# Block products of w_out: seven instead of eight in three of its pairs, on one core

## The reference, cut to what matters

```
y = jnp.concatenate([rmsnorm(y_lru, g_out_lru[i]), rmsnorm(y_attn, g_out_attn[i])], axis=-1)
h = h + y @ w_out[i]
h = h + hier_moe(rmsnorm(h, g_moe[i]), w_rg[i], b_rg[i], w_re[i], b_re[i], w1[i], w3[i], w2[i])
pe = rmsnorm(p[i] @ w_ple[i], g_ple[i])
gate = jax.nn.sigmoid((rmsnorm(h, g_pg[i]) @ w_pg[i]).astype(F32) + b_pg[i].astype(F32))
h = h + (gate * pe.astype(F32)).astype(h.dtype)
```

## Time and profile before

| | |
|---|---|
| time, median of 3 runs | 1372.13 us (1371.0 to 1377.09) |
| time of the profiled execution | 1376.97 us |
| its span on the core | 1375.2 us |
| PE busy | 1094.3 us (80% of the span) |
| DVE busy | 288.5 us (21%) |
| ACT busy | 158.9 us (12%) |
| POOL busy | 53.5 us (4%) |
| bytes read | 473.12 MB, 346 GB/s over the span |

### The profile page before, as it was taken

How to read it: one execution, slowest core, us unless ns; L and a number is a source line. 1 busy time by engine, 2 the same in 40 slices (tenths; PEclk the granted TensorE clock), 3 DMA queues, 4 the chain that set the end, 5 groups by cost and what they waited for, 6 DMA issues and landing times.

```text
span 1375.2 us, 13804 instructions
## 1 busy us (share of the span) xinstructions
PE 1094.3 (80%) x6020; PEld 508.5 (37%) x6020; DVE 288.5 (21%) x443; ACT 158.9 (12%) x315; POOL 53.5 (4%) x66
## 2 busy tenths in 40 slices
PE   8999999999995687666766667666666676899998
PEld 4458887445531233222222223222223222333333
DVE  1204725511341212121221111000000000111116
ACT  1111415002110012000000000000000000110002
POOL 0103100200000002000000000000000000000000
PEclk9999999999898899788898878888878868999999
DMA  9943333364699999999999999999999999999991
GB/s 352 310 153 123 123 123 122 127 248 180 267 384 427 427 427 428 428 430 431 428 426 428 429 426 428 414 427 429 414 428 421 417 427 412 393 397 382 396 353 62
DMA packets 89326, 476.16 MB, mean 346 GB/s; under 512 B 10080, under 2 KB 10224, under 8 KB 67760
## 3 DMA queue, kind: packets, MB, share of 16 engines
q1 hardware_dynamic: 83168, 471.88, 84.8%
q0 software_dynamic: 560, 2.88, 0.6%
q10 hardware_dynamic: 5536, 0.47, 0.3%
HBM read 473.12 MB, written 2.10 MB: 346 GB/s over the span
## 4 chain that ended last, share of the span: by engine, by line
DMA 50%; PE 45%; SPq 3%; DVE 1%; issue 1%; ACT 0%; DVEq 0%
DMA ring<-in_w 49%; PE ps L1457 8%; PE ps L1420 6%; PE ps L1718 6%; PE ps L1798 4%; PE ps L1594 4%; PE ps L1581 4%; PE ps L1895 4%; PE ps L1684 2%; PE ps L1853 2%; SPq L471 1%; PE ps L1677 1%; SPq L462 1%; SPq L389 1%; PE ps L1866 1%
## 5 line engine op out<-in xcount | busy, mean ns | idle before, releaser
L1798 PE MATMUL ps<-ring,area 128*32 128x512 f32 x1024 | 167.7, 805 | 120.7 <-DMA ring<-in_w 119.8
L1718 PE MATMUL ps<-ring,area 128*32 128x512 f32 x976 | 146.4, 719 | 112.5 <-DMA ring<-in_w 112.5
L1209 DVE TENSOR_TENSOR h<-ps,h 128x2048 f32<-128x2048 f32 x32 | 73.3, 2292 | 286.6 <-PE ps L1684 286.6
L1798 PEld LDWEIGHTS ps<-ring,area 128*32 128x32 f32 x1024 | 43.3, 140 | 231.3 <-issue 231.3
L1457 PE MATMUL ps<-hT,ring 128*128 128x256 f32 x512 | 112.9, 380 | 0.0
L1718 PEld LDWEIGHTS ps<-ring,area 128*32 128x32 f32 x976 | 31.4, 122 | 209.0 <-issue 208.6
L1457 PEld LDWEIGHTS ps<-hT,ring 128*128 128x128 f32 x512 | 96.6, 190 | 14.0 <-issue 1.2
L1420 PE MATMUL ps<-ring,hT 128*128 128x512 f32 x192 | 86.0, 608 | 1.1 <-DVE hT L932 1.1
L1895 PE MATMUL ps<-ring,area 128*128 128x512 f32 x176 | 79.8, 595 | 3.5 <-ACT area L896 3.0
L1264 DVE TENSOR_TENSOR hT<-area,ps 128x128 f32<-128x128 f32 x16 | 4.6, 288 | 316.0 <-ACT area L885 316.0
L1677 PE MATMUL ps<-area,hs 128*128 128x128 f32 x512 | 66.8, 286 | 0.5 <-DVE area L1190 0.5
(11 more groups left out here) (285 smaller groups left out, 808.9 us busy)
## 6 DMA issues: line engine op xcount, KB each, us to landing
ring<-in_w SPq DMA_DIRECT2D x126, 2048.0 KB, 20.7
ring<-in_w SPq DMA_DIRECT2D x63, 1024.0 KB, 15.4
ring<-in_w SPq DMA_DIRECT2D x14, 4096.0 KB, 25.2
ring<-in_w_in SPq DMA_DIRECT2D x28, 1024.0 KB, 12.3
ring<-in_w_out SPq DMA_DIRECT2D x16, 1024.0 KB, 7.3
ring<-in_w_pg SPq DMA_DIRECT2D x11, 1024.0 KB, 14.2
area<-in_w SPq DMA_DIRECT2D x2, 2048.0 KB, 14.3
hs<-in_w SPq DMA_DIRECT2D x4, 1024.0 KB, 14.4
```

Of the source, the lines that this page charges most:

```text
L1209: dve.tensor_tensor(h[:, t, :], ps[:, bank:bank + 4, :].rearrange("p b n -> p (b n)"), h[:, t, :], ALU.add).then_inc(acc_done, 1)
L1718: ins = mm(ps[SLOTS * g:SLOTS * g + SLOTS, 0, :], XG[:, b, k, SLOTS * e:SLOTS * e + SLOTS], s[:, D_EXP * kk:D_EXP * kk + D_EXP], start=(k ...
L1798: ins = mm(ps[SLOTS * g:SLOTS * g + SLOTS, 0, :], XG[:, b, k, SLOTS * e:SLOTS * e + SLOTS], s[:, D_EXP * kk:D_EXP * kk + D_EXP], start=(k ...
```

## The change

Three quarters of `w_out` are cut into pairs of column groups: pair 0 is part B with n = 0 and 1, pair 1 part B with n = 2 and 3, pair 2 part A with n = 0 and 1. A pair is a 2 x 2 by 2 x 2 block product (two row tiles t, two halves of 512 inner rows, two column groups), made with Strassen's method (in its form with shared differences) from seven block products of four matmuls each instead of eight. What the products read is made beforehand: four differences of `w_out`'s blocks (128x2048 each) and four of `y`'s (128x512 each). DVE makes those of pairs 0 and 2 (`w_difference`, L1140 to L1147) and all of `y`'s (`y_differences`, L1155 to L1160); POOL makes pair 1's, and the last one of pair 0 (L601 to L615). Each product is added to one, two or three pieces of `h`: 14 additions a pair (`add_products`, L1178; `steps_` lists product, tile, group and the earlier addition to wait for) instead of four (two groups by two tiles). Column groups 2 and 3 of part A stay as they were (L1741).

Line numbers above 1700 on PE, 1130 to 1240 on DVE and 590 to 620 on POOL in this section are those of the changed kernel. SP's load of the first ahead place moves behind the next ring load, since the differences lie in that place until pair 2 is done. A pair's four chunks are freed together, by the first matmul of the next pair. At the end, eight of the logits' blocks of t = 1 are moved ahead of the last transposes (L1757, L1763).

```diff
-                if p_ == 1:
-                    for a in range(2):
-                        expert_load(1, a, ahead_places[a], ahead_loaded[a])
+                if p_ in (1, 2):
+                    expert_load(1, 2 - p_, ahead_places[2 - p_], ahead_loaded[2 - p_])
...
+            pool.wait_ge(chunks_used, WIN_CHUNKS)
+            w_arrived(pool, 1)
+            b11, b12, b22 = w_block(1, 0, 0), w_block(1, 0, 1), w_block(1, 1, 1)
+            pool.tensor_tensor(w_sums[1][:, 0, :], b22, b12, ALU.subtract).then_inc(made_pool, 1)
+            pool.wait_ge(made_pool, 1)
+            pool.tensor_tensor(b12, b12, b11, ALU.subtract).then_inc(made_pool, 1)
+            pool.wait_ge(made_pool, 2)
+            first_b21 = w_last(pool, 0)
+            pool.wait_ge(made_dve, 3)
+            pool.tensor_tensor(first_b21, first_b21, w_sums[0][:, 1, :], ALU.subtract).then_inc(made_pool, 1)
+            pool.tensor_tensor(w_sums[1][:, 1, :], b22, b12, ALU.subtract).then_inc(made_pool, 1)
             pool.wait_ge(lru_act, 4)
...
+            b21 = w_last(pool, 1)
+            pool.wait_ge(made_pool, 4)
+            pool.tensor_tensor(b21, b21, w_sums[1][:, 1, :], ALU.subtract).then_inc(made_pool, 1)
             pool.wait_ge(msBA_ready, 2)
...
+            def y_differences(j, count):
+
+                if j:
+                    dve.wait_ge(products_ps, PRODUCTS + 6)
+                low, high = [y_block(j, t, 0) for t in range(NT)], [y_block(j, t, 1) for t in range(NT)]
+                dve.tensor_tensor(y_sums[:, 0, :, :], low[1], high[1], ALU.add).then_inc(made_dve, 1)
+                dve.tensor_tensor(y_sums[:, 2, :, :], low[0], low[1], ALU.subtract).then_inc(made_dve, 1)
...
+            w_difference(0, 0, 1)
+            w_difference(0, 1, 2)
+            w_difference(0, 2, 3)
+
+            def add_products(j, first, last):
+
+                steps_ = ((0, 0, 0, 0), (0, 0, 1, 0), (0, 1, 0, 0), (0, 1, 1, 0), (1, 0, 0, 1),
+                          (2, 0, 1, 2), (2, 1, 0, 3), (2, 1, 1, 4), (3, 0, 1, 6), (3, 1, 1, 8),
+                          (4, 1, 0, 7), (4, 1, 1, 10), (5, 0, 1, 9), (6, 1, 0, 11))
+                for i, t, n, earlier in steps_[first:last]:
+                    dve.wait_ge(products_ps, PRODUCTS * j + i + 1)
...
+            dve.wait_ge(gates_ps, CB)
+            y_differences(0, 3)
+
 
             dve.wait_ge(gates_ready, CB)
             dve.tensor_tensor(t2, t2, xc, ALU.mult)
...
+            add_products(0, 0, STEPS)
+            w_difference(2, 0, 8)
+            w_difference(2, 1, 9)
+            w_difference(2, 2, 10)
+            dve.wait_ge(lru_act, 4)
+            dve.tensor_reduce(ysum, t1.rearrange("p c t -> p t c"), AX, ALU.add).then_inc(made_dve, 1)
+            add_products(1, 0, 12)
+            dve.wait_ge(ssA_ps, 1)
+            dve.tensor_scalar(ss[:, 4:6], ps[:, 0, 0:NT], 1.0 / D_LRU, EPS, ALU.mult, ALU.add).then_inc(msBA_ready, 1)
+            add_products(1, 12, 13)
+            dve.wait_ge(made_pool, 4 + CB)
+            y_differences(2, 11)
+            add_products(1, 13, STEPS)
             dve.wait_ge(rBA_ready, 2)
...
+            def product(j, i, y, w, frees=0):
+
+                m = PRODUCTS * j + i
+                if 2 <= m < 6:
                     pe_.wait_ge(gates_ready, CB)
-                if n == 3:
-
-                    pe_.wait_ge(hB_ready, 1)
-                    pe_.wait_ge(ysum_ready, 1)
+                elif 6 <= m < 8:
+                    pe_.wait_ge(block_copied, 2 * CB)
+                elif m >= 8:
+                    j_, i_ = divmod(m - 8, PRODUCTS)
+                    pe_.wait_ge(pieces_added, STEPS * j_ + READ_BY[i_])
+                for kk in range(4):
+                    ins = mm(ps[:, product_bank(m), :], y[:, kk, :], w[:, 512 * kk:512 * kk + 512],
+                             start=(kk == 0), stop=(kk == 3))
...
+                product(j, 4, y_sums[:, 2, :, :], w_sums[j][:, 0, :])
+                if j == 1:
+                    pe_.wait_ge(made_dve, 11)
+                    pe_.wait_ge(pieces_added, STEPS)
                     for t in range(NT):
-                        ins = mm(ps[:, 2, t:t + 1], ysum[:, P * t:P * t + P], ones_c[:, 0:1], start=True, stop=True)
+                        ins = mm(ps[:, 0, t:t + 1], ysum[:, P * t:P * t + P], ones_c[:, 0:1], start=True, stop=True)
                     ins.then_inc(ssA_ps, 1)
...
+            pair(0)
+            pair(1)
+            pe_.wait_ge(msBA_ready, 2)
+            pe_.wait_ge(made_pool, 4 + CB)
+            pair(2)
...
+            w_out_A(1, 3)
+            logits(1, 0, 8)
             turn_h(1, 3)
             pe_.wait_ge(xnT_act, 7)
-            logits(1, 0, 12)
+            logits(1, 8, 12)
```

More of the change, by code:

```diff
@@ L352, in ring4, with y_block, w_block, wait_piece @@
             return ring[:, slot, :].rearrange("p (k n) -> p k n", k=4)
+        y_sums = hs_flat[:, 0:2048].rearrange("p (w k m) -> p w k m", w=4, k=4)
+        w_sums = [part(10264, 2 * CH, 2, CH), hT_flat.rearrange("p (w n) -> p w n", w=2), part(10264, 2 * CH, 2, CH)]
+        def y_block(j, t, half):
+            return (yT if j < 2 else gt)[:, 4 * half:4 * half + 4, P * t:P * t + P]
+        def w_block(j, half, n):
+            return ring[:, (pair_chunk(j) + 2 * n + half) % RING, :]
+        def wait_piece(engine, t, n):
+            if n < 2:
+                engine.wait_ge(pieces_added, ADDED - STEPS + WHOLE_BY[t, n])
+            else:
+                engine.wait_ge(h_ready, 2 * t + n - 1)
+        def w_arrived(engine, j):
+            for half, n in ((0, 0), (0, 1), (1, 1)):
+                c = pair_chunk(j) + 2 * n + half
+                engine.wait_ge(loaded[c % RING], 16 * (c // RING + 1))
+        def w_last(engine, j):
+            c = pair_chunk(j) + 1
+            engine.wait_ge(loaded[c % RING], 16 * (c // RING + 1))
+            engine.wait_ge(products_ps, PRODUCTS * j + 2)
+            return w_block(j, 1, 0)
         block = ctx.enter_context(nc.Block())
@@ L1066, in _, with w_difference @@
             dve.tensor_scalar(ss[:, 6:8], ss[:, 6:8], 1.0 / (HEADS * HD), EPS, ALU.mult, ALU.add).then_inc(msBA_ready, 1)
+            def w_difference(j, which, count):
+                b11, b12, b22 = w_block(j, 0, 0), w_block(j, 0, 1), w_block(j, 1, 1)
+                dve.wait_ge(made_dve, count - 1)
+                if which == 0:
+                    w_arrived(dve, j)
+                    ins = dve.tensor_tensor(w_sums[j][:, 0, :], b22, b12, ALU.subtract)
+                elif which == 1:
+                    ins = dve.tensor_tensor(b12, b12, b11, ALU.subtract)
+                elif which == 2:
+                    ins = dve.tensor_tensor(w_sums[j][:, 1, :], b22, b12, ALU.subtract)
+                else:
+                    b21 = w_last(dve, j)
+                    ins = dve.tensor_tensor(b21, b21, w_sums[j][:, 1, :], ALU.subtract)
+                ins.then_inc(made_dve, 1)
@@ new lines, in _ @@
+            w_difference(0, 0, 1)
[7 more added lines that the diff above has]
+                    dve.wait_ge(products_ps, PRODUCTS * j + i + 1)
+                    if earlier or j:
+                        dve.wait_ge(pieces_added, STEPS * j + earlier)
+                    col = 512 * (2 * (j % 2) + n)
+                    piece = h[:, t, col:col + 512]
+                    scale = (6 if j < 2 else 4) + t
+                    dve.scalar_tensor_tensor(out=piece, in0=ps[:, product_bank(PRODUCTS * j + i), :],
+                                             scalar=rstd[:, scale:scale + 1], in1=piece, op0=ALU.mult, op1=ALU.add
+                                             ).then_inc(pieces_added, 1)
@@ L1122, in _ @@
+            dve.wait_ge(pieces_added, ADDED)
+            add_A(0, 2)
+            add_A(0, 3)
             root_mean(0)
@@ new lines, in arrived, with pair @@
+            def arrived(j, half, n):
+                chunk(pair_chunk(j) + 2 * n + half)
+                return w_block(j, half, n)
+            def pair(j):
+                product(j, 0, y_block(j, 0, 0), arrived(j, 0, 0), 4 * (j > 0))
+                product(j, 1, y_block(j, 0, 1), arrived(j, 1, 0))
+                if j == 0:
+                    pe_.wait_ge(made_dve, 7)
+                elif j == 1:
+                    pe_.wait_ge(made_pool, 4)
+                else:
+                    pe_.wait_ge(made_dve, 15)
+                product(j, 2, y_sums[:, 1, :, :], w_sums[j][:, 1, :])
+                product(j, 3, y_sums[:, 0, :, :], arrived(j, 0, 1))
+                product(j, 4, y_sums[:, 2, :, :], w_sums[j][:, 0, :])
+                if j == 1:
+                    pe_.wait_ge(made_dve, 11)
+                    pe_.wait_ge(pieces_added, STEPS)
@@ L1587, in w_out_A @@
-            def w_out_A(t, n):
+                product(j, 5, y_sums[:, 3, :, :], arrived(j, 1, 1))
+                if j == 0:
+                    pe_.wait_ge(made_pool, 3)
+                elif j == 1:
+                    pe_.wait_ge(made_pool, 5 + CB)
+                else:
```

(8 more changed lines are left out.)

157 lines of the change are left out of this document (74 added, 83 removed).

## The result

| | before | after |
|---|---|---|
| time, median of 7 runs | 1372.13 us (1371.0 to 1377.09) | 1378.94 us (1377.77 to 1379.42) |
| ratio to before | | 1.0037 [1.0021, 1.0053] |
| profiled execution, its span | 1376.97, 1375.2 us | 1378.94, 1377.0 us |
| PE busy | 1094.3 us | 1078.2 us |
| DVE busy | 288.5 us | 345.3 us |

What follows compares the result with a forecast made beforehand. PE bounds the kernel to about 380 us, then the stream of experts' weights. Part A's end +6.8 us (saved products against waits and clock), less 0.8 for the logits, gives +6.0 on 1372.1: 1378.1 us, range 1365 to 1384.

Steps and rivals of the forecast that it cites:

- The mechanism: POOL's four differences and DVE's LRU chain alternate at SBUF; chain ends at 264.5 instead of 251.4 us; chance 0.60.
- What is added on DVE ahead of the chain: `y`'s differences delay the chain's start by 1.5 us, partly absorbed; reciprocal ends at 238.1 instead of 237.7 us.
- -10.3 us by fewer products: On PE, 12 groups by tile (82.4 us) become 21 block products (72.1 us): 10.3 us less.
- The first wait: PE's ninth product waits 7.1 us for pair 0's fourth addition, late behind the chain.
- The second wait: PE waits 8.0 us for `ysum`, done at 289.0 us behind three differences and POOL's fifth.
- The step behind it: PE ends pair 1: 1.1 us wait for additions and mean, 1.1 us for the clock; pair 2 starts at 298.3.
- slower, by the clock: Rival: PE's three waits each bring the lower clock, lasting into pair 2; +9.4 us, 1381.5 us; chance 0.14.
- Part A: Pair 2 takes 24.0 us and the rest 35.7; part A ends at 358.0 against 351.2 us, +6.8.
- The tail: Logits at the end cover the last addition and turn: 0.8 us less (0.5 to 1.7).
- From gather to end: Each us by which the experts' first gather (near 369 us) begins earlier or later moves the end by one.
- No lock that matters: Rival: DVE and POOL share ports or POOL gives way; PE waits about nothing, 1362 us; chance 0.16.
- DVE keeps the ports: Rival: DVE's next instruction precedes waiting POOL; chain ends at 255.7 us, PE waits 6.9 us, total 1368 us; chance 0.10.

Runs made afterwards that it cites:

- e1: Changed kernel with POOL's five differences cut to 8 of 2048 columns: 2307.04 us, with other routing, so only the part ahead of the routing is comparable.
- e3: e2 with POOL's second and fourth differences held until DVE's chain ends, and pair 0's last difference made by DVE: 1361.87 us, 0.9909 of before.
- e4: Kernel before plus four unused two-input POOL subtractions of 128x2048 at the place of the four differences: 1372.22 us, 0.9999 of before.
- e2: Changed kernel with DVE making `ysum` right behind pair 0's additions, and pair 2's three differences behind pair 1's additions and the mean: 1369.09 us, 0.9962 of before.
- e7: e3 with the logits of tile 1 in the old order, all twelve behind the last transposes: 1361.83 us, 0.9929 of before.
- e9: The same kernel as e3, run again in five rounds: 1362.36 us, 0.9917 of before.
- e8: e3 with the changed kernel's order on DVE, pair 2's three differences ahead of `ysum`: 1366.27 us, 0.9942 of before.
- b_third: The kernel before, unchanged, run for a third profile: 1371.07 us, span 1369.1 us.
- e6: Kernel before with only the logits' new order, eight blocks of tile 1 ahead of the last transposes: 1372.38 us over 11 runs, 0.9996 of before.
- b_again: The kernel before, unchanged, run for a second profile: 1376.65 us.

## Why the prediction was right

**The mechanism.** POOL's differences and the LRU's chain take turns at SBUF, so the chain ends late, and PE, which reads additions from the ninth product on, waits. e1 and e3 remove it from two sides (POOL's work away; POOL's work later) and both waits vanish; e4 has POOL's work alone, without the products, and shows the chain stretched. The chain was to end at 264.5 us and ended at 263.8. The price of one POOL instruction, 4.46 us, was measured as 4.53. (The 4.497 us of the Trainium skill, GPSIMD Engine Reference, section Elementwise — side-by-side cycle accounting, lies nearer still.)

**What is added on DVE ahead of the chain.** Right: the reciprocal was to end at 238.1 us and did (in e2's profile, too, it runs its 12.95 us beside POOL).

**-10.3 us by fewer products.** Right: the pairs of e3 take 72.5 us with the mean, and the kernel is faster than before by 0.9% as soon as nothing waits.

**The first wait.** 7.1 us said, 6.5 measured: the additions came 0.7 us earlier.

**The second wait.** 8.0 said, 5.2 measured. PE came to L1719 at 282.5 instead of 281.0, since the ninth product ran at the lower level (5.56 instead of 3.60 us), which I had let the second wait hide; and so it did, by a shorter wait. `ysum` came at 287.6 instead of 289.0: 0.7 us from the chain, 0.3 from L615, which holds DVE for 4.2 instead of 4.5 us, the rest from smaller ones.

**The step behind it.** I had a wait of 1.1 us for the mean and 1.1 us for the clock. There was no wait, and the clock cost 3.4 us (L1719 1.01 instead of 0.50, the two products 9.98 instead of 7.11). With `ysum` 1.4 us earlier the start of pair 2 came out at 298.4 where 298.3 was said. That this agrees to 0.1 us is two errors against each other: the rival "slower, by the clock" had its mechanism partly right, and what the second wait took off, the clock gave back. Over all, waits and clock held up the pairs by 17.3 us, 11.7 of them waits; the forecast had 17.3 too, 16.2 of them waits. So the clock's term was mis-sized: 1.1 us said and 3.4 measured behind the second wait, and 2.0 more behind the first, which only shortened the second wait.

**Part A.** It ended at 358.3 us (358.0 said). But the 35.7 us from pair 2 to there were taken from a profile with the lower clock in them, and the changed kernel's profile has as much, 322.4 to 358.3. e3 has 34.2 for the same work (304.05 to 338.27), and so have e2, e7 and e9, while e8 has the longer time again. Why the changed kernel's profile has it is open; the forecast had no ground to expect it. Against the earlier trace rows the end of part A moved by 7.1 us (6.8 said); against b_third it is +9.0 (358.30 - 349.31): 0.3 already at the start of `w_out`, -10.3 + 17.3, and 1.7 at the lower level in part A's end. In pair 2 PE waited for nothing, as said.

**The tail.** -0.8 said. From the end of part A to the gather it is 9.25 us instead of b_third's 10.37, so -1.1 in this profile, and -0.8 in e6. As a gain of the whole time it isn't seen: e6 and e7 show no median moved. This term was mis-sized, by its 0.8 us; what it left out is the clock at the gather, which the new order mostly has at the lower level (above).

**From gather to end.** The long pieces of DMA keep their place against the end. The changed kernel's chain, start, us, what:

```profile
367.55 3.81 PE ps L1822 x32
...
417.54 29.94 DMA ring<-in_w
```

First long piece and span are 417.54 and 1377.0 here, 415.75 and 1375.2 in the earlier trace rows, 409.69 and 1369.1 in b_third, 400.35 and 1359.7 in e3: 959.35 to 959.46 us apart (958.7 to 960.5 over all profiles but e1's). That one us counts as one is right, within that spread. SP's later load of the first ahead place cost nothing, as said: from the gather to this piece the changed kernel takes as long as b_third. But from the gather to this piece it isn't constant: 49.99 us after a gather of 3.81 us (b_third 50.01), 52.5 to 53.1 after one at a lower clock (before, e2, e3, e6). The gather was forecast near 369 and came at 367.6; the prediction's +6.0 put it against 362.82 of a profile whose clock was low. For the same reason the span of about 1381 us that it gave for the profile is missed by 4: it is 1377.0. Measured against b_third the gather is +7.9 (-1.1 in the tail on the 9.0), 1.9 more than forecast, most of it the 1.7 of part A's end, which the forecast had in both kernels. b_third is 1.1 us below the median of 1372.13: +6.8, as the medians say. So the mechanism is the forecast's and so is the sum of waits and clock, but that 1378.1 lies within 0.8 us of 1378.94 is in part chance.

**The rivals.** "No lock that matters" is excluded by L1196 to L1199. "DVE keeps the ports" isn't what happened where it mattered: in the chain POOL took every second turn. "Slower, by the clock" stays as above.

## What to carry to other kernels

POOL and DVE don't work side by side where DVE's instructions read two SBUF tensors: the large two-input POOL instructions beside this chain put nearly their whole time into it, 4.2 of 4.5 us each. Put them beside instructions of DVE's that one sees unhindered in the trace (here the reciprocal and the additions from PSUM), and what is awaited first ahead of what is only due. Moving `ysum` ahead of pair 2's differences, and three of POOL's differences out of the chain, turned a kernel that was 0.4% slower into one that is 0.9% faster, without a matmul less.

Before costing a difference of some us, have a profile of the kernel before whose own time lies near the median. The 1.8 us between the two spans shown here are 6.8 in the medians, and a second profile alone, b_again, would not have told.

## What I had not expected of the hardware

Turns: with both engines always wanting SBUF, neither goes twice (L603, L1196, L607, L1197, L608, the scan; the same in e2 and e4, and in e8 scaling by scaling). At 118.84 us of the earlier trace rows it is otherwise: DVE's small L994 stands from 118.30 us, and POOL's L538 begins at 118.84 and takes no more than its 0.73 us, ahead of it. So the turns are shown for the instructions above and are no rule for all; what is different at 118.84 is open.

Two groups of times in the kernel before: of 56 runs in four sets 36 lie at 1370.5 to 1373.4 us and 20 at 1375.2 to 1378.0, with nothing between. The profiles of the upper group (before, b_again) have PE at the lower level from 355 to 365 us, over the last logits and the gather, and begin the stream of weights at 415.5 to 415.8 instead of 409.7 us; part of the 6 us (1.7) is lost ahead of it, in part A's last turn and group. e7 with the old order of the logits has both groups, e6 with the new one no time above 1374.4 in 11 runs. The lower level at the gather alone doesn't make the upper group: e6's profile has it and is the shortest of its eleven. That the clock's level makes the groups is read from three profiles and these two experiments, and not shown by a change of the clock alone; why one execution gets the lower level at that place and the next doesn't is open.
